# Moving every low-part subtraction of a two-block transformer kernel from GpSimd to VectorE

## The reference, cut to what matters

```python
h = layernorm(x, emb_ln_g, emb_ln_b)
for l in range(2):                         # hybrid_layer
    proj = h @ w_in[l]                     # 2048 x 4160, then the mixers
    h = layernorm(ALPHA * h + mix @ w_out[l] + b_out[l], ln_g[l], ln_b[l])
x = h + 0.5 * swiglu(rms_norm(h, ffn1_norm), ffn1_gate, ffn1_up, ffn1_down)
x = x + mixer(rms_norm(x, mix_norm), rms_norm(mem, mem_norm)) @ w_out_2
x = x + 0.5 * swiglu(rms_norm(x, ffn2_norm), ffn2_gate, ffn2_up, ffn2_down)
```

## Time and profile before

| | |
|---|---|
| median of three runs | 2868.55 us (2863.43 to 2869.46) |
| profiled execution, first to last instruction | 2865.5 us |
| mean granted TensorE clock, share of full speed | 0.971 |
| busy: TensorE matmuls / VectorE / ScalarE / GpSimd | 94% / 62% / 48% / 42% |
| instructions | 41336 |

### The profile page before, as it was taken

One profiled execution on the slowest core, in us unless ns is written; L12 is line 12 of the kernel. 1 busy time (PEld: TensorE's weight loads), 2 busy tenths in 40 slices (PEclk: granted clock), 3 DMA queues, 4 the chain that ended last, 5 costly groups with the idle time before them and its releaser, 6 DMA issues.

```text
span 2865.5 us, 41336 instructions
## 1 busy us (share of the span) xinstructions
PE 2686.7 (94%) x14642; PEld 2286.1 (80%) x14642; DVE 1768.5 (62%) x2504; ACT 1365.0 (48%) x2009; POOL 1204.2 (42%) x556
## 2 busy tenths in 40 slices
PE   6699999799999699999999998887999999999999
PEld 5587788687787588888888876776788888888888
DVE  7866668657559877733444445888567763344432
ACT  4455553455543544444444443655554444444443
POOL 3533334533344444444444443222344444444444
PEclk8899999899999799999999998999999999999999
DMA  5344344344344254555544552333445445555454
GB/s 223 118 155 164 148 162 163 131 159 162 146 175 163 90 189 179 179 183 206 189 178 180 172 203 104 122 114 112 153 170 194 179 174 189 200 185 190 177 176 160
DMA packets 72778, 474.01 MB, mean 165 GB/s; under 512 B 8288, under 2 KB 8672, under 8 KB 28128
## 3 DMA queue, kind: packets, MB, share of 16 engines
q1 hardware_dynamic: 72672, 472.60, 45.8%
HBM read 469.43 MB, written 2.10 MB: 165 GB/s over the span
## 4 chain that ended last, share of the span: by engine, by line
PE 77%; DVE 18%; issue 2%; ACT 2%; POOL 1%; DMA 0%; SPq 0%; ACTq 0%; DVEq 0%; POOLq 0%
PE acc L661 49%; PE acc L662 24%; DVE low L1131 3%; DVE normed L1233 1%; PE score L872 1%; DVE scale_c L1404 1%; DVE moment L1235 1%; DVE moment L1243 1%; ACT high L938 1%; POOL xs L1647 1%; DVE x L1178 1%; DVE normed L1557 1%; DVE square_l L1391 1%; DVE moment_sq L1241 1%; DVE feat L1406 0%
## 5 line engine op out<-in xcount | busy, mean ns | idle before, releaser
L1620 POOL TENSOR_TENSOR low<-raw,high 128x1024 fp32r<-128x1024 f32 (+2 forms) x488 | 1139.1, 2334 | 1591.6 <-ACT high L938 1591.6
L661 PE MATMUL acc<-xs,high 128*128 128x512 f32 x4544 | 1649.5, 406 | 64.0 <-POOL xs L1647 31.4
L662 PE MATMUL acc<-xs,low 128*128 128x256 f32 x4544 | 1287.4, 283 | 0.0
L938 ACT ACTIVATE high<-raw 128x1024 fp32r<-128x1024 f32 (+2 forms) x976 | 944.4, 975 | 560.6 <-PE acc L662 509.2
L661 PEld LDWEIGHTS acc<-xs,high 128*128 128x128 f32 x4544 | 867.7, 191 | 295.5 <-issue 44.5
L662 PEld LDWEIGHTS acc<-xs,low 128*128 128x128 f32 x4544 | 872.6, 192 | 1.5
L1131 DVE TENSOR_TENSOR low<-raw,high 128x1024 fp32r<-128x1024 f32 (+1 forms) x488 | 650.6, 1333 | 340.1 <-ACT high L938 313.4
L661 PE MATMUL acc<-hidden,high 128*128 128x512 f32 x1408 | 497.7, 399 | 0.0
L964 ACT ACTIVATE lowsum<-acc 128x256 f32<-128x256 f32 x444 | 169.8, 383 | 600.2 <-PE acc L662 599.4
L662 PE MATMUL acc<-hidden,low 128*128 128x256 f32 x1408 | 395.4, 281 | 0.0
L661 PEld LDWEIGHTS acc<-hidden,high 128*128 128x128 f32 x1408 | 264.6, 188 | 66.1
(11 more groups left out here) (240 smaller groups left out, 1858.6 us busy)
## 6 DMA issues: line engine op xcount, KB each, us to landing
raw<-w_up_dram SPq DMA_DIRECT2D x176, 1024.0 KB, 4.8
raw<-w_down_dram SPq DMA_DIRECT2D x128, 704.0 KB, 4.0
raw<-w_in_dram SPq DMA_DIRECT2D x80, 1024.0 KB, 4.8
raw<-w_out_dram SPq DMA_DIRECT2D x32, 1024.0 KB, 4.8
raw<-w_heads_dram SPq DMA_DIRECT2D x24, 1024.0 KB, 4.8
raw<-w_mixout_dram SPq DMA_DIRECT2D x16, 1024.0 KB, 4.8
raw<-w_nat_dram SPq DMA_DIRECT2D x8, 1024.0 KB, 4.8
raw<-w_uq_dram SPq DMA_DIRECT2D x8, 768.0 KB, 4.4
```

Source lines behind the costliest of these rows:

```text
L661: eng.matmul(bank_[:, :], hi, moving, start=start, stop=False)
L662: return eng.matmul(bank_[:, S:2 * S], lo, moving[:, 0:S], start=False, stop=stop)
L938: eng.activation(high[:, s % SPLIT, piece * 8 * P:(8 * piece + n) * P], raw[:, s % RAW, at_:at_ + n * P], ACT.Copy).then_inc(highs, 1)
L1620: eng.tensor_tensor(low[:, s % SPLIT, w], raw[:, s % RAW, w], high[:, s % SPLIT, w].bitcast(F32), ALU.subtract).then_inc(lows_a, 1)
```

## The change

All low parts of weights and of activations are made by VectorE. `FILLS` and the two semaphores `split_l["g"]` and `split_l["v"]` become one semaphore with one count. VectorE's `split_low` takes the piece as an argument; each slot now also makes the low part of the first piece of the slab after the next, ahead of the tile's store (in regions that store several tiles in a slot, ahead of the second tile of uq, the third of pool, the fifth of uk, and behind the stores of uv). The low parts of normalised tiles follow the normalisation of the next group of `CUTS`. GpSimd keeps only the 16 squares of ln1. The wait of `first_sum` on GpSimd's low parts of mem goes away. The core of the diff:

```diff
-FILLS = {"mem": "gv", "emb": "gg", "ln0": "gg", "ln1": "vv", "mix": "gv", "ffn2": "vv"}
+SPLIT_NORMS = ("mem", "emb", "ln0", "ln1", "mix", "ffn2")
...
+def split_count(name, kt):
+
+    return KT * SPLIT_NORMS.index(name) + kt + 1
...
         def wait_split(eng, name, kt):
-            who, n = low_count(name, kt)
-            eng.wait_ge(split_l[who], n)
+            eng.wait_ge(split_l, split_count(name, kt))
...
@block.vector
-            def split_low(r, k, i):
+            def split_low(piece, r, k, i):
                 s = r.s0 + k
-                w = slice(8 * P, (8 + r.pieces[1]) * P)
-                eng.wait_ge(highs, val(2 * s + 2, 8, i))
+                n, at_ = r.pieces[piece], piece * r.pieces[0] * P
+                w = slice(piece * 8 * P, (8 * piece + n) * P)
+                eng.wait_ge(highs, val(2 * s + 1 + piece, 8, i))
...
             def slot(r, k, i):
                 nxt = following(r, k, i)
+                if r.name == "mem_k" and k == 0:
+                    split_low(0, *nxt)
                 if nxt and not (k == 0 and r.name in TOGETHER):
-                    split_low(*nxt)
+                    split_low(1, *nxt)
                 for step in steps_at(r, k, i):
                     do(*step)
-                for tile, per, prod_, pper in tiles_done(r, k, i):
+                nxt = nxt and following(*nxt)
+                done = tiles_done(r, k, i)
+                early = {"tile": 0, "down": 0, "natural": 0, "uq": 1, "uk": 4, "pool": 2}.get(r.kind, -1)
+                for nth, (tile, per, prod_, pper) in enumerate(done):
+                    if nxt and nth == early:
+                        split_low(0, *nxt)
                     store(r, k, i, tile, per)
+                if nxt and not 0 <= early < len(done):
+                    split_low(0, *nxt)
...
-                    if name == "emb":
-
-                        eng.wait_ge(split_l["g"], low_count("mem", KT - 2)[1])
...
-            def low_and_squares(n):
+            def low_and_squares(name, n):
 
                 for kt in range(*CUTS[n]):
-                    split_low_of("ln1", kt, "ffn1_g")
-                if n > 1:
+                    if name != "ln1" and kt % 2:
+                        eng.wait_ge(embedded_v, KT // 2 * LAYER_NORMS.index(name) + kt // 2 + 1)
+                    split_low_of(name, kt, "ffn1_g" if name == "ln1" else None)
+                if name == "ln1" and n > 1:
...
-                        if name == "ln1" and n:
-                            low_and_squares(n - 1)
+                        if n:
+                            low_and_squares(name, n - 1)
...
+                    low_and_squares(name, len(CUTS) - 1)
                     if name == "ln1":
-                        low_and_squares(len(CUTS) - 1)
...
@block.gpsimd
-            def split_low(r, k, i):
...
-            walk(eng, slot, between)
+            for kt in range(KT):
+
+                eng.wait_ge(embedded, kt + 1)
+                eng.tensor_tensor(square[:, kt, :], x[:, kt, :], x[:, kt, :], ALU.mult).then_inc(squared, 1)
```

More of the change, by code:

```diff
@@ L1125, in _ @@
             step_ = chain.step
[L1127 removed]
+            def split_low(piece, r, k, i):
                 s = r.s0 + k
[L1129 to L1132 removed]
+                n, at_ = r.pieces[piece], piece * r.pieces[0] * P
+                w = slice(piece * 8 * P, (8 * piece + n) * P)
+                eng.wait_ge(highs, val(2 * s + 1 + piece, 8, i))
+                eng.tensor_tensor(low[:, s % SPLIT, w], raw[:, s % RAW, at_:at_ + n * P], high[:, s % SPLIT, w].bitcast(F32),
+                                  ALU.subtract).then_inc((lows_a, lows_b)[piece], 1)
             def slot(r, k, i):
                 nxt = following(r, k, i)
+                if r.name == "mem_k" and k == 0:
+                    split_low(0, *nxt)
                 if nxt and not (k == 0 and r.name in TOGETHER):
[L1137 removed]
+                    split_low(1, *nxt)
                 for step in steps_at(r, k, i):
                     do(*step)
[L1140 removed]
+                nxt = nxt and following(*nxt)
[4 more added lines that the diff above has]
+                        split_low(0, *nxt)
                     store(r, k, i, tile, per)
+                if nxt and not 0 <= early < len(done):
+                    split_low(0, *nxt)
             def store(r, k, i, tile, per):
@@ L1280, in split_low_of @@
                 else:
[L1281 to L1282 removed]
+                    y = x if name in LAYER_NORMS else normed
+                    ins = eng.tensor_tensor(xs[:, kt, S:2 * S], y[:, kt, :], hi, ALU.subtract)
+                ins.then_inc(split_l, 1)
             def rotate(a, b, c, s_, out, out_b, count):
@@ L1615, in _ @@
         def _(eng):
-            def split_low(r, k, i):
-                s = r.s0 + k
-                w = slice(0, r.pieces[0] * P)
-                eng.wait_ge(highs, val(2 * s + 1, 8, i))
-                eng.tensor_tensor(low[:, s % SPLIT, w], raw[:, s % RAW, w], high[:, s % SPLIT, w].bitcast(F32),
-                                  ALU.subtract).then_inc(lows_a, 1)
-            def slot(r, k, i):
-                nxt = following(r, k, i)
-                if nxt and not (k == 0 and norms_before(r.name)):
-                    split_low(*nxt)
-            def between(name):
-                if name == "mem_k":
-                    split_low(REG[name], 0, None)
-                if norms_before(name):
-                    split_low(REG[name], 1, None)
-                for n in norms_before(name):
-                    y = x if n in LAYER_NORMS else normed
-                    for kt in range(KT):
-                        who, _ = low_count(n, kt)
-                        if n == "ln1":
-                            eng.wait_ge(embedded, kt + 1)
-                            eng.tensor_tensor(square[:, kt, :], x[:, kt, :], x[:, kt, :], ALU.mult).then_inc(squared, 1)
-                        if who == "g":
-                            eng.wait_ge(split_h, high_count(n, kt))
-                            if n in LAYER_NORMS and kt % 2:
-                                eng.wait_ge(embedded_v, KT // 2 * LAYER_NORMS.index(n) + kt // 2 + 1)
-                            eng.tensor_tensor(xs[:, kt, S:2 * S], y[:, kt, :], xs[:, kt, 0:S].bitcast(F32),
-                                              ALU.subtract).then_inc(split_l["g"], 1)
-            walk(eng, slot, between)
+            for kt in range(KT):
+                eng.wait_ge(embedded, kt + 1)
+                eng.tensor_tensor(square[:, kt, :], x[:, kt, :], x[:, kt, :], ALU.mult).then_inc(squared, 1)
 class Chain:
```

22 lines of the change are left out of this document (6 added, 16 removed).

## The result

The changed kernel took 2776.79 us in the median of four executions (2772.96 to 2790.42), the kernel before 2866.77 us. The ratio is 0.9701, 95% interval 0.9672 to 0.9729.

What follows compares the result with a forecast made beforehand. VectorE, stalled by GpSimd, was taken to bound all but the feed-forward, where TensorE is full; 6.5 + 10.2 + 6 + 0 + 2.8 + 16.2 + 12 = 53.7 us off 2868.55 gave 2814 us, range 2787 to 2847.

Steps and rivals of the forecast that it cites:

- Rival B: Stalls are VectorE's own waits, not GpSimd's doing; about 2930 us, decided by L1404 staying over 1.83 us; chance 0.05.
- rival A: Heads chain doesn't shorten because TensorE or ScalarE is next in line; about 2837 us, chance 0.20.
- rival C: No change: norms lose earlier wins and heads only trades stalls for low parts; within 6 us of 2868, chance 0.05.
- the rest: Head norms in in_a0, uv and pool stores, nat0 decay sums, lower-clock matmuls: 12 us, taken between 0 and 20.
- low end: 2787 us: the rest at 20 us, 3 us at the start, 10 us from full clock in heads, a few more.
- Heads and nat1: Chain of VectorE's operations: 45.8 us of stalls go, 29.6 us of first pieces are added, net 16.2 us won.
- The start: Up to the first LayerNorm: stalls of 20.4 us go, 14.9 us added, 1 us from beginning sooner; 6.5 us earlier.
- out0 and out1: TensorE's waits for VectorE's stores go, 10.2 us, and gaps at the regions' ends shrink, 6 us.
- stores: In out0 and out1, all 10.2 us of TensorE's waits for VectorE's stores go; at worst half stays.
- ends: End of out0 and out1: gap ahead of the mean's matmul falls from 5.61 to 2.3 us; 6 us for both.
- The norms: emb and ln0: VectorE alone comes out even, 0 us, between 1 us won and 5 us lost for each.
- Slab 2: Its low part, behind twelve tiles on GpSimd, held TensorE for 1.40 us; that goes twice, 2.8 us.

Runs made afterwards that it cites:

- dummy_heads: Changed kernel, with GpSimd also subtracting constants nobody reads, twice per slab in heads and nat1; heads took 223.4 us, nat1 47.5.
- undo_mem: Changed kernel with the 8 first pieces of mem_k and mem_v back on GpSimd; one execution, in_a0 started at 97.6 us.
- weights_only: Kernel before, with only the weights' first pieces moved to VectorE, GpSimd keeping its share of activations' low parts; 2787.79 us, ratio 0.9745.

## Why the prediction was wrong, point by point

- **The mechanism was right.** GpSimd's subtractions made VectorE's instructions stand still, and a first piece costs VectorE 1.14 us. dummy_heads shows the first without any low part being late. Rival B falls with L1404 (L1401 after) at 0.692 us, rival A with heads at 193.2 instead of 212.1 us, rival C with the rest.
- **The step that failed: TensorE's own busy time was taken as fixed.** In the prediction's words, "Nothing that VectorE or GpSimd does there shows in the time", with 5.65 us a slot and 0 us for the feed-forward; and the time at the lower clock stands only inside "the rest", 12 us. The sum was 53.7 us, the two profiled spans differ by 89.3: 35.6 us short. TensorE's gaps fell from 178.8 to 123.8 us, by 55.0, which is about the sum. The other 34.3 us are TensorE's busy time for the same 14642 matmuls, 2686.7 us before and 2652.4 after. That 55.0 is so close to 53.7 is in part luck, since "the rest" was a guess that held gaps and clock in one.
- **Of the 34.3 us, 12.5 are in the first half of the feed-forward**, which is 13.0 us shorter. In before VectorE, held by GpSimd, delivered a low part 0.16 us late, and behind it TensorE was in the slower rhythm for the rest of the half. In other executions of the changed kernel both halves were in the faster rhythm, or neither. Without these 13 us the profiled execution would lie at about 2791 us, just inside the range, so which side of the low end an execution falls on is chance.
- **Heads and nat1, 16.2 us forecast, 25.6 measured.** The sum took VectorE's stalls less its added pieces. TensorE's gaps fell by 19.1 us (46.3 to 27.2). The other 6.5 are TensorE's own busy time, 213.13 us before and 206.63 after, at a mean granted clock of 0.94 and 0.97; busy time times clock is 200 us in both. The prediction had this only under "the rest" and in its low end (10 us). The two stretches, before and then after:

```profile
1762.90:2022.30 259.40, 213.13 (x1091) 180.00 (x1089) 194.06 (x303) 139.96 (x241) 70.99 (x28) 0.94 0.31 115
```

```profile
1701.50:1935.30 233.80, 206.63 (x1090) 174.96 (x1089) 176.46 (x331) 139.81 (x241) 0.00 (x0) 0.97 0.35 126
```

- **The start, 6.5 forecast, 10.4 measured**: TensorE's gaps fell by 7.7 us and its busy time by 2.7, at a clock of 0.85 before and 0.89 after. By cause, undo_mem gives 7.0 of the 10.4 to eight pieces, weights_only 1.3 to the activations. VectorE's busy time fell by 7.4 us (79.58 to 72.19), where the sum of stalls less added work was 5.5.
- **out0 and out1, 16.2 forecast (stores 10.2, ends 6), 21.4 measured**: the waits were forecast well. Those for the stores fell from 10.2 to 0.3 us, those ahead of the mean's matmul from 10.8 to 4.8, and TensorE's gaps by 16.3 in all. The other 5.1 us are again busy time, at a clock of 0.93 and 0.96 before and 0.96 and 0.97 after.

The start and out0 after, as in the earlier trace rows:

```profile
13.00:90.60 77.60, 53.73 (x238) 41.74 (x236) 72.19 (x125) 33.07 (x51) 0.00 (x0) 0.89 0.55 207
395.70:498.40 102.70, 92.60 (x521) 79.39 (x519) 89.46 (x142) 44.21 (x58) 0.00 (x0) 0.96 0.50 180
```

- **The norms, 0 forecast**: in_a0 and in_a1 are 1.5 and 0.9 us longer in weights_only than after; that step was right. **Slab 2, 2.8 forecast**: TensorE's waits for GpSimd's low parts of weights, 4.9 us in three places before, are gone.
- **The rest, 12 forecast, 13.4 with slab 2 of in_a0**: 16.6 by regions, within its bounds of 0 to 20.

So the gaps were priced about right, and what was left out was that TensorE's matmuls themselves get shorter: outside the feed-forward by the granted clock when gaps close, in it by the rhythm when nothing interrupts. The regions outside the feed-forward all won more than forecast, by 20 to 60%.

## What to carry to other kernels

Where VectorE is near its limit, look beside an instruction with two SBUF inputs that takes several times as long in some places as in others (here 2.76 and 0.69 us): if GpSimd runs there, its work is paid twice, and VectorE may well do it itself. Closing a gap of TensorE can win more than the gap, so compare TensorE's busy time of the same matmuls too, not its gaps alone. A wait of a fraction of a microsecond on TensorE can cost far more than its own length, so count matmuls in equal stretches at full clock before calling a stretch fixed. Where executions of one kernel fall into steps, compare regions, not medians.

## What the runs showed of the hardware that was not expected

TensorE, without gaps and at full clock, repeated the same pair of matmuls every 347 or every 353 ns (579 or 568 matmuls in 100 us). In these traces it kept one of the two until the next interruption, and an interruption as small as one matmul of 32 columns or a matmul 0.16 us late was enough for a change, though not each one made a change. Over a feed-forward half the difference is 13 us. Behind 33 of 34 matmuls of 32 columns came the faster rhythm; behind 64, 112 and 128 columns came either, and without odd matmuls it varied from one execution to the next. What inside TensorE makes the difference was not found out.
